# The recurrent mixer on compact operands: two 64x64 products at the diagonal quarters in place of one block-diagonal 128x128 product

## The chip, the cores and the metric

One core of one Trainium2 chip runs the whole program. The metric is the device time of one execution in microseconds. Smaller is better. Three executions of the kernel before gave a median of 4775.67 us.

## The reference, cut to what matters

The program is two layers of one kind (not touched here) and then a second block. In the second block one of the two branches is a recurrent mixer with 16 heads of 64 channels, run forwards and backwards over 768 tokens (256 of context, 512 of the sequence). Per head and per direction it computes, token by token (`w` is the decay, `a` and `b` the rank-one correction, `k`, `v`, `r` as usual):

```
S_t = S_(t-1) * w_t  +  (S_(t-1) a_t) b_t^T  +  v_t k_t^T        # 64 x 64 state of a head
y_t = S_t r_t                                                    # 64 outputs, used for the 512 tokens of x
```

The outputs of both directions are added, normalised per head, a bonus term is added, and the result is gated. The kernel computes this in chunks of 64 tokens: inside a chunk a triangular system is solved, between chunks a 64x64 state per head is carried. All operands of this part are f32.

## The kernel before, in words

`rwkv_phase` (L1896 on) does the recurrent mixer. Two heads share the 128 partitions, so 16 heads make 8 pairs, and with two directions there are 16 units. One unit has 12 chunks (`NCH`), of which the first 4 (`CCH`) are context and give no output. The loop over `ITERATIONS` runs a software pipeline: in one iteration unit u is built (`solve`, `fill`), unit u-1 is scanned (`scan`), unit u+1 is prepared on VectorE and ScalarE (`prepare`, `open_lora`, `exps`), and the operations of a pair of heads (`norm_product`, `tile_product`, `final_product`) are spread over even and odd iterations. Each iteration has 36 slots. The order of the work on each engine is written out slot by slot: in each slot TensorE does `solve`, then `fill` (slots 3 to 11), then `scan`, then at most one operation of the others. Everything waits on counted semaphores.

What each part does in a unit:

- `solve`: in slots 0 to 2 the gram products of four chunks each (L2062, against `qr`: 64 columns for context chunks, 128 for the others). Then five levels of the triangular solve. A level takes six slots: three batches of four products (L2079), which ScalarE copies out of PSUM (L2272), and three batches of four products (L2090), which VectorE merges under a mask (L2444, L2447) and turns (L2464). That is 60 products of each of the two kinds in a unit.
- `fill`: four gram products with k (L2105), then four transposes of `wb` (L2110), four of `wk` (L2115), for each of three batches.
- `scan`: three slots for each of the 12 chunks. Slot one makes W (L2130, and L2133 against the state), ScalarE copies it (L2288). Slot two makes N (L2137), ScalarE copies it (L2291) and also scales the old state (L2295). Slot three makes the state's increment (L2154, L2157), and VectorE combines it with the scaled old state (L2412, L2415). For the 8 output chunks slot three has three products more (L2148, L2149, L2160). They give rows of outputs, which VectorE copies or adds (L2475, L2478) and TensorE turns back once for each pair of heads (L2225).

Every product of two heads is one product of the full 128x128 array: the stationary operand holds the two heads at its diagonal quarters and zeros elsewhere (`wb`, `wk`, `wq`, `wV`, `wAT`, `wBT`, `wS` and so on). The zeros are set once by GpSimd (L1860) in the phase before, and the wide copies keep them. An f32 product is two records in the trace (two weight loads and two matmuls). An f32 transpose is one record of each.

Of the kernel before, what the change touches and what calls it, by code (L numbers as in the profile page):

```python
# [15 lines left out]
P = 128  # L16
# [1775 lines left out]
class MixerSpill(Side):  # L1792
# [5 lines left out]
        "heads_spilled", "constants_loaded", "zeroed", "share_kept", "mean_ready", "root_taken", "inverse_ready", "rows_scaled"]  # L1798
# [9 lines left out]
    def bind(self, landed, *sems):  # L1808
        self.landed = landed
        self.slot_spilled = sems[:self.SLOTS]  # L1810
        (self.heads_spilled, self.constants_loaded, self.zeroed, self.share_kept, self.mean_ready, self.root_taken, self.inverse_ready,
         self.rows_scaled) = sems[self.SLOTS:]
# [42 lines left out]
    def gpsimd(self, pool):  # L1855
# [3 lines left out]
        for n in ("wb", "wk", "wq", "wV"):  # L1859
            nc.gpsimd.memset(R[n][:], 0.0).then_inc(self.zeroed, 1)  # L1860
# [7 lines left out]
        pool.wait_ge(self.zeroed, 4)  # L1868
# [27 lines left out]
def rwkv_phase(nc, T, R, lora, gd, ob_d, weights, chunks, last_stored):  # L1896
# [12 lines left out]
    qr, wq, wb, wk, wV = R["qr"], R["wq"], R["wb"], R["wk"], R["wV"]  # L1909
    X, U, wAT, Y = R["X"], R["U"], R["wAT"], R["Y"]  # L1910
    wBT, wbt, wkt, Cc, Dd = R["wBT"], R["wbt"], R["wkt"], R["C"], R["D"]
    wS, wP, wW, wN, pl = R["wS"], R["wP"], R["wW"], R["wN"], R["pl"]
    bonus, rk, rows, yb, sq, ob = R["bonus"], R["rk"], R["rows"], R["yb"], R["sq"], R["ob"]
# [4 lines left out]
    def flat(ap):  # L1918
        return ap.rearrange("p h t -> p (h t)")

    def flat4(ap):
        return ap.rearrange("p c h t -> p (c h t)")

    def wide4(ap):
        return ap.rearrange("p c (o t) -> p c o t", o=1).to_broadcast([P, 4, 2, L_CH])

    def level(d, lv):
        return cst["level"][:, d, lv, :].bitcast(U32).rearrange("p (c h t) -> p c h t", c=1, h=2).to_broadcast(
            [P, 4, 2, L_CH])

    def strict(d):
        return cst["strict_wide"][:, d, :].rearrange("p (c h t) -> p c h t", c=1, h=2).to_broadcast([P, 4, 2, L_CH])

    def incl(d):
        return cst["incl"][:, d, :].rearrange("p (c t) -> p c t", c=1).to_broadcast([P, 4, L_CH])

    def four(bank):
        return psum[:, bank, :].rearrange("p (c h t) -> p c h t", c=4, h=2)

    def r_slot(u):  # L1940
        return 1 + u % 3

    def two(ap, u, c):

        return ap[:, u % 2, c:c + 2].rearrange("p c t -> p (c t)")

    def slot_of(ap, u):
        return ap[:, u % 2]
# [23 lines left out]
    PRESET_AT = {16: 0, 27: 1, 35: 2}  # L1972
    preset_order = ((0, 1, 2), (0, 2, 1))

    def solve_step(k):
# [6 lines left out]
             "s_ready", "y_ready", "norm_sums", "bonus_sums", "v_turned", "rows_turned", "mean_ready", "var_ready",  # L1982
             "gate_ready",
             "opened", "exps_ready", "q_widened", "y_preset", "u_copied", "bt_copied", "kt_copied", "w_copied",
             "n_copied", "s_copied", "s_decayed", "squared", "norm_roots", "v_copied", "ln_root",
             "sums_ready", "less_ready", "b_ready", "a_ready", "k_ready", "q_ready", "r_ready", "wb_ready", "wk_ready",
             "pl_ready", "y_opened", "at_ready", "d_ready", "x_opened", "x_done", "y_back", "y_final", "gram_k_read",
             "y_taken", "kr_ready", "kk_ready", "rk_ready", "bonus_ready", "yb_ready", "centred", "sq_ready",
             "normed", "inverse_ready", "ln_inverse", "scaled", "added", "ob_ready", "pads_zero", "weights_loaded"]
    with Phase(nc, names) as (  # L1990
            block, rk_loaded, v_loaded, up_loaded, ob_stored0, ob_stored1,
            lora_up, gram_b, gram_k, b_turned, k_turned, u_ready, z_ready, w_ready, n_ready,
            s_ready, y_ready, norm_sums, bonus_sums, v_turned, rows_turned, mean_ready, var_ready,
            gate_ready,
            opened, exps_ready, q_widened, y_preset, u_copied, bt_copied, kt_copied, w_copied,
            n_copied, s_copied, s_decayed, squared, norm_roots, v_copied, ln_root,
            sums_ready, less_ready, b_ready, a_ready, k_ready, q_ready, r_ready, wb_ready, wk_ready,
            pl_ready, y_opened, at_ready, d_ready, x_opened, x_done, y_back, y_final, gram_k_read,
            y_taken, kr_ready, kk_ready, rk_ready, bonus_ready, yb_ready, centred, sq_ready,
            normed, inverse_ready, ln_inverse, scaled, added, ob_ready, pads_zero, weights_loaded):  # L2000
        ob_stored = (ob_stored0, ob_stored1)

        @block.gpsimd
        def _(pool):
            nc.gpsimd.memset(qr[:, :, N_ALL:], 0.0).then_inc(pads_zero, 1)
            nc.gpsimd.memset(Cc[:, :, XCH, :], 0.0).then_inc(pads_zero, 1)
            nc.gpsimd.memset(Dd[:, :, XCH, :], 0.0).then_inc(pads_zero, 1)
# [38 lines left out]
        def _(pe):  # L2046
            def solve(k, u):

                g, d = divmod(u, 2)
                if k < 3:  # L2050
                    b = k
                    pe.wait_ge(wb_ready, 2 * u + 2)
# [4 lines left out]
                    for i in range(4):  # L2057
                        c = 4 * b + i
                        at = slice(c * L_CH, (c + 1) * L_CH)
                        rhs = qr[:, 0, at] if c < CCH else qr[:, 0:r_slot(u) + 1:r_slot(u), at]  # L2060
                        n = L_CH if c < CCH else P
                        last = nc.tensor.matmul(psum[:, b, i * P:i * P + n], flat(wb[:, c]), rhs, start=True, stop=True)  # L2062
# [6 lines left out]
                if step == 0:  # L2069
# [7 lines left out]
                    for i in range(4):  # L2077
                        c = 4 * b + i
                        last = nc.tensor.matmul(psum[:, b, i * P:(i + 1) * P], flat(wAT[:, c]), flat(X[:, c]),  # L2079
                                                start=True, stop=True)  # L2080
                    last.then_inc(u_ready, 1)
                else:
# [3 lines left out]
                    for i in range(4):  # L2086
                        c = 4 * b + i
                        y = flat(Y[:, u % 2, c])
                        l_, r_ = (y, flat(U[:, c])) if lv < LEVELS else (flat(U[:, c]), y)
# [157 lines left out]
            for i in ITERATIONS:  # L2247
                build, scanned, prep, norm, tile, final = stages(i)
                for k in range(SLOTS_):
# [4 lines left out]
                    if scanned is not None:  # L2254
                        scan(k, scanned)
# [1403 lines left out]
```

## Time and profile before

| | us |
|---|---|
| median of three executions | 4775.67 |
| lowest and highest | 4772.65, 4778.11 |
| span of the profiled execution | 4773.1 |
| of it: stretch 2070 to 3170, the recurrent mixer | 1100 |
| one pair of units in it (two iterations) | 130.2 |

The profiled execution is one run, 2.6 us under the median. A row of the profile names the line, the engine, the operation and its tiles, how often it occurs, its busy time as a union over time, and the mean duration of one. PE is TensorE's matmuls, PEld its weight loads, DVE is VectorE, ACT is ScalarE, POOL is GpSimd. Matmuls overlap in the pipeline, so the duration of one (275 ns) is longer than the distance from one to the next.

### The profile page before, as it was taken

Reading aid. Unit: us, or ns where it says so; the run is one execution under the profiler, and the core shown is the slowest. Engines: PE = TensorE matmul, PEld = TensorE weight load, DVE = VectorE, ACT = ScalarE, POOL = GpSimd, SP = SyncE. Lnnn points to the kernel's source line nnn. Section 1 sums busy time; section 2 is a strip of 40 time slices with the busy share of each in tenths; the row PEclk is TensorE's granted clock in tenths of the full one; section 3 lists DMA queues with packets and bytes.
Section 4 is the critical chain, followed back from the end, with each engine's and each line's share of the span. In section 5 each row is a group of like instructions: output and inputs, shape, how many; then the busy total and the mean of one; then the engine's idle time right before and its main releaser. Section 6 shows DMA issues by size and latency. Waiting matters only on the chain. (4 is left out here: it accounts for less than half of the span.)

```text
span 4773.1 us, 57369 instructions
## 1 busy us (share of the span) xinstructions
PE 4295.2 (90%) x20622; PEld 3153.4 (66%) x20622; DVE 3084.4 (65%) x6230; ACT 1654.8 (35%) x3360; POOL 850.6 (18%) x866
## 2 busy tenths in 40 slices
PE   8989999989998999989999999989899887777777
PEld 6657887747887877879888888968644333333332
DVE  5664434674434767567777777634577888888885
ACT  3354233353242356135555455432211111111111
POOL 1101010101011012000000000000134444444443
PEclk9999999999998999989999999989999988999989
DMA  4213433213433102310000000033599999999998
GB/s 131 67 40 128 146 124 98 82 40 106 148 126 117 62 18 97 103 36 12 15 11 7 15 15 15 1 132 111 197 388 416 421 413 413 413 411 415 409 415 345
DMA packets 150587, 794.50 MB, mean 166 GB/s; under 512 B 19880, under 2 KB 23192, under 8 KB 83488
## 3 DMA queue, kind: packets, MB, share of 16 engines
q0 software_dynamic: 84544, 575.18, 29.9%
q1 hardware_dynamic: 58272, 188.32, 12.0%
q10 hardware_dynamic: 7488, 27.30, 1.8%
q8 instruction: 169, 2.77, 0.2%
q14 instruction: 114, 0.93, 0.1%
HBM read 766.53 MB, written 20.00 MB: 165 GB/s over the span
## 5 line engine op out<-in xcount | busy, mean ns | idle before, releaser
L3255 PE MATMUL psum<-rows,diag 128*128 128x512 f32 x2048 | 1003.6, 640 | 228.1 <-ACT diag L3134 209.4
L3255 PEld LDWEIGHTS psum<-rows,diag 128*128 128x128 f32 x2048 | 408.3, 204 | 779.8 <-issue 766.8
L2996 DVE SCALAR_TENSOR_TENSOR uh<-rows,h_rows 128x1024 f32<-128x1024 f32 x512 | 628.3, 1227 | 205.1 <-DMA rows<-in_peer_uv,sel_idx 178.6
L2953 POOL DMA_INDIRECT rows<-in_peer_uv,sel_idx x512 | 611.2, 1194 | 739.0 <-PE psum L3255 677.4
L529 DVE TENSOR_TENSOR w_split_lo<-w_raw,w_split_hi 128x1024 fp32r<-128x1024 f32 (+1 forms) x271 | 325.0, 1209 | 498.8 <-ACT w_split_hi L516 494.7
L516 ACT CAST w_split_hi<-w_raw 128x1024 fp32r<-128x1024 f32 (+1 forms) x271 | 276.5, 1028 | 616.2 <-PE psum L465 397.3
L3127 ACT ACTIVATE g<-g 128x4 f32<-128x4 f32 x128 | 26.3, 205 | 1090.2 <-DVE g L3007 1090.2
L2079 PE MATMUL psum<-x,wAT_wide 128*128 128x128 f32 x1920 | 254.5, 276 | 1.4 <-DVE x L2444 1.0
L2079 PEld LDWEIGHTS psum<-x,wAT_wide 128*128 128x128 f32 x1920 | 237.4, 192 | 18.4 <-issue 15.0
L693 POOL TENSOR_TENSOR uT_lo<-normed_rows,uT_hi 128x512 fp32r<-128x512 f32 x64 | 90.2, 1409 | 664.8 <-ACT uT_hi L669 664.8
L465 PE MATMUL psum<-hT_mlp_hi,w_split_hi 128*128 128x512 f32 x512 | 201.1, 393 | 4.7 <-DVE hT_mlp_lo L261 4.6
L2090 PE MATMUL psum<-x,Y_wide 128*128 128x128 f32 x1536 | 202.1, 275 | 0.0
L465 PE MATMUL psum<-hT_mlp_hi,w_split_lo 128*128 128x512 f32 x512 | 200.3, 391 | 0.0
L465 PE MATMUL psum<-hT_mlp_lo,w_split_hi 128*128 128x512 f32 x512 | 200.2, 391 | 0.0
L465 PE MATMUL psum<-w_split_hi,uT_hi 128*128 128x512 f32 x512 | 199.2, 389 | 0.0
L465 PE MATMUL psum<-w_split_lo,uT_hi 128*128 128x512 f32 x512 | 199.2, 389 | 0.0
L465 PE MATMUL psum<-w_split_hi,uT_lo 128*128 128x512 f32 x512 | 199.2, 389 | 0.0
L2650 POOL DMA_DIRECT2D merge_stage<-hT_spill x7 | 3.7, 538 | 1094.9 <-POOLq L190 1090.7
L2090 PEld LDWEIGHTS psum<-x,Y_wide 128*128 128x128 f32 x1536 | 189.4, 192 | 10.8 <-issue 9.8
L2272 ACT COPY x<-psum 128x512 f32<-128x512 f32 x240 | 140.6, 586 | 156.0 <-PE psum L2079 152.5
L3134 ACT ACTIVATE diag<-ident_sb,g 128x128 f32<-128x128 f32 x512 | 163.5, 390 | 36.7 <-DVE g L3012 36.7
L2412 DVE SCALAR_TENSOR_TENSOR wS<-psum,pl,wP 128x128 f32<-128x128 f32 x160 | 54.9, 343 | 170.5 <-PE psum L2157 170.4
(538 smaller groups left out, 9356.7 us busy)
## 6 DMA issues: line engine op xcount, KB each, us to landing
w_raw<-in_w_in SPq DMA_DIRECT2D x105, 512.0 KB, 4.3
w_raw<-in_w_up SPq DMA_DIRECT2D x64, 512.0 KB, 4.2
w_raw<-in_w_down SPq DMA_DIRECT2D x64, 512.0 KB, 4.2
amask_sb<-in_w_mod ACTq DMA_DIRECT2D x48, 512.0 KB, 4.5
wq<-in_peer_wq SPq DMA_DIRECT2D x24, 512.0 KB, 7.7
rows<-in_peer_uv,sel_idx POOLq DMA_INDIRECT x512, 12.6
qkpad<-in_w_out SPq DMA_DIRECT2D x12, 512.0 KB, 5.1
w_raw<-in_w_out SPq DMA_DIRECT2D x12, 512.0 KB, 3.9
```

The source lines that it names most:

```text
L465: last = nc.tensor.matmul(psum[0:rows, bank, 0:cols], l_, r_, start=(start and c == 0 and j == 0), stop=(stop and c == len(pairs) - 1 and ...
L516: nc.scalar.copy(ring.hi[:, q % SPLIT_RING, :, 0:w], slot(q)[:, :, 0:w]).then_inc(hi_ready, 1)
L529: nc.vector.tensor_tensor(ring.lo[:, q % SPLIT_RING, :, 0:w], slot(q)[:, :, 0:w], ring.hi[:, q % SPLIT_RING, :, 0:w].bitcast(F32), ALU.sub ...
L693: return nc.gpsimd.tensor_tensor(uT.lo[:, k, :], squares[:, k % 2, :], uT.hi[:, k, :].bitcast(F32), ALU.subtract)
L2079: last = nc.tensor.matmul(psum[:, b, i * P:(i + 1) * P], flat(wAT[:, c]), flat(X[:, c]), start=True, stop=True)
L2090: last = nc.tensor.matmul(psum[:, b, i * P:(i + 1) * P], l_, r_, start=True, stop=True)
L2272: nc.scalar.copy(flat4(U[:, batch(b)]), psum[:, b, :]).then_inc(u_copied, 1)
L2412: nc.vector.scalar_tensor_tensor(wS[:], psum[:, 5, 0:P], scale, wP[:], ALU.mult, ALU.add).then_inc(s_copied, 1)
L2953: nc.gpsimd.indirect_dma_start(out=rows[:, n % RB, :], out_offset=None, in_=I["peer_uv"], in_offset=bass.IndirectOffsetOnAxis(ap=sel[:, t, ...
L2996: nc.vector.scalar_tensor_tensor(prod[:], rows[:, n % RB, 0:D], 1.0, h[:, t, :], ALU.mult, ALU.mult, accum_out=dots[:, (n // BATCH) % 2, s ...
L3134: nc.scalar.activation(diag[:, n % (2 * BATCH), :], ident[:], ACT.Copy, scale=g2[:, b % 2, i:i + 1]).then_inc(diag_ready, 1)
L3255: last = nc.tensor.matmul(psum[:, 2 * (t % 2) + half, :], diag[:, n % (2 * BATCH), :], rows[:, n % RB, D + half * NB:D + (half + 1) * NB], ...
```

## The change

Each product of two heads becomes two products of 64x64 operands (`by_head`): partitions 0 to 63 against 0 to 63, and partitions 64 to 127 against 64 to 127. No operand holds the zero quarters any more, so every tile of the mixer is half as wide and the copies, masks and turns work on 256 columns where they worked on 512.

- The gram products, the solve and the scan use `by_head`. The transposes of `wb` and `wk` become `by_head` products against an identity (`cst["eye"]`).
- The state's decay: one more product (identity against the old state) adds the old state in PSUM, and ScalarE scales the sum while it copies it. VectorE's `state` and ScalarE's scaling of the old state are gone.
- The outputs are made channels first, with `vv`, the state and N as stationary operands, and are accumulated over both directions in PSUM bank 6. The rows, their copies and their turning are gone. ScalarE copies bank 6 once for each pair of heads.
- ScalarE's widening of q and its presets of Y are gone. GpSimd presets Y. GpSimd's zeroing is gone.
- In each slot TensorE and ScalarE do `scan` ahead of `solve`. `qr` and `Ss` have more buffers, and some waits on `y_done` and `n_copied` are new.

```diff
+    def by_head(out, lhsT, rhs, start, stop):
+        for at in halves:
+            last = nc.tensor.matmul(out[at], lhsT[at], rhs[at], start=start, stop=stop)
+        return last
...
         @block.gpsimd
         def _(pool):
-            nc.gpsimd.memset(qr[:, :, N_ALL:], 0.0).then_inc(pads_zero, 1)
...
+            for u in range(UNITS):
+                for j, b in enumerate(scan_order[u % 2]):
+                    if u >= 2:
+                        pool.wait_ge(n_ready, 12 * (u - 2) + 4 * j + 4)
+                    nc.gpsimd.tensor_copy(Y[:, u % 2, batch(b)], mask(cst["eye"])).then_inc(y_preset, 1)
...
-                        last = nc.tensor.matmul(psum[:, b, i * P:i * P + n], flat(wb[:, c]), rhs, start=True, stop=True)
+                        last = by_head(psum[:, b, i * P:i * P + n], wb[:, c], rhs, True, True)
...
-                        last = nc.tensor.matmul(psum[:, b, i * P:(i + 1) * P], flat(wAT[:, c]), flat(X[:, c]),
-                                                start=True, stop=True)
+                        last = by_head(psum[:, b, i * L_CH:(i + 1) * L_CH], AT[:, c], X[:, c], True, True)
...
-                        last = nc.tensor.matmul(psum[:, b, i * P:(i + 1) * P], l_, r_, start=True, stop=True)
+                        last = by_head(psum[:, b, i * L_CH:(i + 1) * L_CH], l_, r_, True, True)
...
-                        last = nc.tensor.transpose(psum[:, 3, i * P:(i + 1) * P], flat(wb[:, 4 * b + i]), ident[:])
+                        last = by_head(psum[:, 3, i * L_CH:(i + 1) * L_CH], wb[:, 4 * b + i], cst["eye"], True, True)
...
-                    last = nc.tensor.matmul(W, flat(wBT[:, u % 2, c]), v, start=True, stop=(n == 0))
+                    last = by_head(W, BT[:, u % 2, c], v, True, n == 0)
...
-                    nc.tensor.matmul(N, flat(Y[:, u % 2, c]), wW[:], start=True, stop=True).then_inc(n_ready, 1)
+                    by_head(N, Y[:, u % 2, c], Ww[:], True, True).then_inc(n_ready, 1)
...
+                        by_head(S_, kt[:, u % 2, c], v, True, False)
+                        if n:
+                            by_head(S_, cst["eye"], Ss[:, n % 2], False, False)
+                        pe.wait_ge(n_copied, 12 * u + n + 1)
+                        by_head(S_, bt[:, u % 2, c], Nn[:], False, True).then_inc(s_ready, 1)
                     if n >= CCH:
...
+                        by_head(y, vv[:, g % 2, c], Cc[:, u % 2, x_], first, False)
+                        by_head(y, Ss[:, n % 2], qr[:, u % 3, 1, at], False, False)
+                        pe.wait_ge(n_copied, 12 * u + n + 1)
+                        by_head(y, Nn[:], Dd[:, u % 2, x_], False, last_).then_inc(y_done, 1)
...
-                    for c in range(XCH):
-                        last = nc.tensor.transpose(psum[:, 7, c * L_CH:(c + 1) * L_CH], rows[:, c * P:(c + 1) * P],
-                                                   ident[0:L_CH, 0:L_CH])
...
-                    nc.scalar.copy(flat4(U[:, batch(b)]), psum[:, b, :]).then_inc(u_copied, 1)
+                    nc.scalar.copy(flat(U[:, batch(b)]), narrow(b)).then_inc(u_copied, 1)
...
-                        nc.scalar.activation(wP[:], wS[:], ACT.Copy, scale=pl[:, u % 3, c:c + 1]
-                                             ).then_inc(s_decayed, 1)
...
+                    act.wait_ge(s_ready, 11 * u + n + 1)
+                    nc.scalar.activation(Ss[:, (n + 1) % 2], psum[:, 5, 0:L_CH], ACT.Copy, scale=pl[:, u % 3, c:c + 1]
+                                         ).then_inc(s_copied, 1)
...
-                    nc.vector.scalar_tensor_tensor(wS[:], psum[:, 5, 0:P], scale, wP[:], ALU.mult, ALU.add
-                                                   ).then_inc(s_copied, 1)
...
-                    nc.vector.copy_predicated(X[:, batch(b)], level(d, lv), four(b)).then_inc(x_done, 1)
+                    nc.vector.copy_predicated(X[:, batch(b)], level(d, lv), cells(narrow(b))).then_inc(x_done, 1)
...
-                    nc.vector.transpose(flat4(Y[:, u % 2, batch(b)]), flat4(X[:, batch(b)])).then_inc(y_back, 1)
+                    nc.vector.transpose(flat(Y[:, u % 2, batch(b)]), flat(X[:, batch(b)])).then_inc(y_back, 1)
```

## Rows read from the trace of the kernel before

**Rows 1.** Page: the span, then busy time, share and records of each engine.
```profile
span 4773.1 us, 57369 instructions
PE 4295.2 (90%) x20622; PEld 3153.4 (66%) x20622; DVE 3084.4 (65%) x6230; ACT 1654.8 (35%) x3360; POOL 850.6 (18%) x866
```

**Rows 2.** Stretches, all engines: start:end, length, busy (records), clock, DMA share, GB/s.
```profile
2070.00:3170.00 1100.00, 1004.20 (x8028) 932.08 (x8028) 791.90 (x1224) 550.28 (x1216) 4.34 (x10) 0.98 0.05 16
...
2662.30:2729.00 66.70, 61.33 (x499) 57.02 (x499) 49.72 (x78) 32.50 (x72) 0.00 (x0) 1.00 0.02 5
2729.00:2792.60 63.60, 60.60 (x502) 57.37 (x501) 48.03 (x74) 35.50 (x81) 0.00 (x0) 1.00 0.07 22
```

**Rows 3.** Timeline of PE in one unit: start, length, line, form, records merged.
```profile
2662.35 1.00 PE L2062 MATMUL psum<-qr,arena 128*128 128x64 f32 x8
2663.19 0.44 PE L2130 MATMUL psum<-arena,wBT_wide 128*128 128x128 f32 x2
...
2666.78 0.60 PE L2180 MATMUL psum<-lora,arena 128*128 128x256 f32 x2
2667.21 1.05 PE L2079 MATMUL psum<-x,wAT_wide 128*128 128x128 f32 x8
...
2671.70 0.60 PE L2110 MATMUL psum<-ident_sb,arena 128*128 128x128 f32 x4
...
2672.36 1.02 PE L2180 MATMUL psum<-lora,arena 128*128 128x512 f32 x2
2673.22 1.05 PE L2079 MATMUL psum<-x,wAT_wide 128*128 128x128 f32 x8
```

**Rows 4.** Timeline around products with 64 stationary rows, then their weight loads' group.
```profile
2684.24 0.39 PE L2133 MATMUL psum<-wS,arena 128*128 128x128 f32 x2
2684.56 0.71 PE L2225 MATMUL psum<-ident_sb,y_rows 64*128 64x64 f32 x8
2685.20 1.05 PE L2079 MATMUL psum<-x,wAT_wide 128*128 128x128 f32 x7
...
L2225 PEld LDWEIGHTS psum<-ident_sb,y_rows 64*128 64x128 f32 x64 | 4.6, 138 | 1.8 <-DVE y_rows L2478 1.0
```

**Rows 5.** Waits, longest in total, over 12 units (2208.1 to 2989.5): total, times, longest.
```profile
PE psum L2133 <- DVE wS L2412: 18.0, 24, 1.4
```

**Rows 6.** Timeline of PE in the last unit, which has no solve beside its scan.
```profile
3117.50 0.49 PE L2133 MATMUL psum<-wS,arena 128*128 128x128 f32 x2 [0.22 <-DVE wS L2412]
3118.34 0.49 PE L2137 MATMUL psum<-wW,Y_wide 128*128 128x128 f32 x2 [0.35 <-ACT wW L2288]
...
3120.12 0.49 PE L2133 MATMUL psum<-wS,arena 128*128 128x128 f32 x2 [0.22 <-DVE wS L2412]
```

**Rows 7.** Groups of VectorE and ScalarE in the mixer: count, busy us, mean ns.
```profile
L2444 DVE COPY_PREDICATED x<-arena,psum 128x512 f32<-128x512 uint32 x192 | 138.1, 719 | 34.1 <-PE psum L2090 33.6
L2464 DVE STREAM_TRANSPOSE Y_wide<-x 128x512 f32<-128x512 f32 x192 | 135.9, 708 | 4.6
L2412 DVE SCALAR_TENSOR_TENSOR wS<-psum,pl,wP 128x128 f32<-128x128 f32 x160 | 54.9, 343 | 170.5 <-PE psum L2157 170.4
...
L2455 DVE TENSOR_TENSOR wBT_wide<-psum,arena 128x512 f32<-128x512 f32 x48 | 32.2, 671 | 14.5 <-PE psum L2105 14.5
...
L2457 DVE TENSOR_TENSOR gate_rows<-psum,arena 128x256 f32<-128x256 f32 x32 | 13.1, 411 | 0.0
...
L2272 ACT COPY x<-psum 128x512 f32<-128x512 f32 x240 | 140.6, 586 | 156.0 <-PE psum L2079 152.5
...
L2321 ACT ACT_TABLE_LOAD x16 | 20.5, 1283 | 5.8 <-DVE arena L2527 5.6
```

**Rows 8.** GpSimd: the zeroing before the mixer, and the nearest copy-like operation.
```profile
1869.12 7.91 POOL L1860 MEMSET arena<- 128x1536 f32 x4
1883.38 0.57 POOL L1863 DMA_DIRECT2D zr_spill<-z_ring  x1 [6.34 <-DVE z_ring L3390]
...
L693 POOL TENSOR_TENSOR uT_lo<-normed_rows,uT_hi 128x512 fp32r<-128x512 f32 x64 | 90.2, 1409 | 664.8 <-ACT uT_hi L669 664.8
```

More of the change, by code:

```diff
@@ L1908, in rwkv_phase @@
     kk, kr, nrm, dec, Lc, eR, aa = (R[n] for n in ("kk", "kr", "nrm", "dec", "Lc", "eR", "aa"))
[L1909 to L1913, printed above, removed]
+    qr, wb, wk, vv = R["qr"], R["wb"], R["wk"], R["v"]
+    X, U, AT, Y = R["X"], R["U"], R["AT"], R["Y"]
+    BT, bt, kt, Cc, Dd = R["BT"], R["bt"], R["kt"], R["C"], R["D"]
+    Ss, Ww, Nn, pl = R["S"], R["W"], R["N"], R["pl"]
+    bonus, rk, yb, sq, ob = R["bonus"], R["rk"], R["yb"], R["sq"], R["ob"]
+    halves = (slice(0, 64), slice(64, P))
     def cells(ap):
@@ L2249, in _ @@
                 for k in range(SLOTS_):
+                    if scanned is not None:
+                        scan(k, scanned)
                     if build is not None:
@@ L2381, in _ @@
                 for k in range(SLOTS_):
+                    if scanned is not None:
+                        scan(k, scanned)
                     if build is not None:
@@ L2385, in _ @@
                             fill(k, build)
-                    if scanned is not None:
-                        scan(k, scanned)
-                    if build is not None and k in (1, 3):
-                        widen_q(k // 2, build)
                     if prep and k in (0, 2, 4, 6):
@@ L2393, in _ @@
                         exps(k, prep)
-                    if prep is not None and k in PRESET_AT:
-                        preset(PRESET_AT[k], prep)
                     if tile is not None and k in TURNED_AT:
@@ L2603, in _ @@
                         solve(k, build)
-                    if scanned is not None and k % 3 == 2 and k < SLOTS_ - 1:
-                        state(k // 3, scanned)
                     if build is not None:
@@ L2609, in _ @@
                             fill(k, build)
-                    if scanned is not None and k in (24, 35):
-                        outputs(k // 35, scanned)
                     if tile is not None and k in (6, 11):
@@ L2717, in rwkv_constants @@
     incl = [(row <= col), (row >= col)]
-    out["strict_wide"] = np.stack([np.tile(m, (1, 2)) * out["ones"] for m in strict], 1).astype(f)
+    out["strict"] = np.stack(strict, 1).astype(f)
     out["incl"] = np.stack(incl, 1).astype(f)
@@ L2725, in rwkv_constants @@
         lev[:, 1, i] = 1.0 * (same & ((row // m) % 2 == 0) & ((col // m) % 2 == 1))
-    out["level"] = np.tile(lev, (1, 1, 1, 2)) * out["ones"][:, None, None, :]
+    out["level"] = lev
+    out["eye"] = (row == col).astype(f)
     tt = np.arange(N_ALL)
@@ L3367, in second_block_program @@
         for n in ("wb", "wk"):
-            R[n] = share.take([NCH, 2, L_CH])
-        for n in ("wq", "wV"):
-            R[n] = share.take([2, NCH, 2, L_CH])
+            R[n] = share.take([NCH, L_CH])
+        R["v"] = share.take([2, NCH, L_CH])
         loads = [(cst[n][:], I["rwc_" + n]) for n in cst] + [
```

260 lines of the change are left out of this document (97 added, 163 removed).

## The prediction

> **What bounds the kernel now.** The page is read first: PE is busy for 90% of the span, but that is an average over stages [rows 1]. The table of stretches then shows the stage that the change touches. It lasts 1100 us and has PE busy for 1004 of them, DVE for 792 and ACT for 550, with a clock of 0.98 and nearly no DMA [rows 2]. Within it two iterations, one pair of units, take 66.7 + 63.6 = 130.3 us, so one unit takes 65.15 us. PE is busy for 61.0 of these at the full clock, DVE for 48.9, ACT for 34.0 [rows 2]. The mixer is bound by PE. The phases before and behind it are separated by barriers and their code stays the same, so the whole effect is what a unit gains or loses, times 16.
>
> The timeline prices what PE does. Eight full products take 1.05 us with the last record's 0.275 in it, so one record starts 0.111 us behind the other and a product of two records costs 0.223 [rows 3]. A full transpose has one record and costs (0.60 - 0.27) / 3 = 0.109 [rows 3]. The lora product with 512 columns takes 0.86 and the one with 256 takes 0.43, start to start [rows 3]. A gram product with only 64 moving columns is no cheaper: eight records take 0.84 from start to start, 0.105 each [rows 3]. So at 64 columns it is the load of 128 stationary columns that sets the pace, and narrowing the moving side alone gains nothing.
>
> With these the unit adds up. The products of a unit are 24 gram, 60 + 60 in the solve, 23 for W, 12 for N, 22 for the state and 24 for the outputs, 225 in all: 225 x 0.223 = 50.2 us. The 24 transposes make 2.6, the four lora products 2 x (0.86 + 0.43) = 2.6. The operations of a pair of heads are five products of 512 columns and one of 256 (norms, bonus, final ones: 5 x 0.86 + 0.43 = 4.7) and 12 transposes (1.3), so 6.0, or 3.0 for a unit. Turning the output rows back takes 2685.20 - 2684.46 = 0.74 for a pair, 0.4 for a unit [rows 4]. The sum is 58.8 us. The measured 65.15 leaves 6.3 us of waits and restarts. The main named wait is W's second product on VectorE's state, 18 us over 12 units with single waits of 1.4 [rows 5].
>
> **The change part by part.**
>
> Number of records. A full product becomes two of 64x64, each of two records. So 0.223 us becomes the price p of four short records. It is counted as follows: 8 gram products with 64 columns, 120 of the solve, 24 former transposes, 23 of W, 12 of N, 22 + 10 of the state (the identity product is new, for all but the first and last chunk) and 24 of outputs make 243 pairs at p. The 16 gram products with 128 moving columns cost q.
>
> The price p. No row shows two quarters of the array at work, so it is bounded. Above: the records follow one another. The nearest row is the turning with 64 stationary rows and 64 moving columns. Its weight loads are busy for 4.6 us in 8 groups of 8, so (0.575 - 0.138) / 7 = 0.062 apart [rows 4], and p = 4 x 0.062 = 0.248. The column count gives nearly the same: 0.43 for two records of 256 columns is 0.054 for 64 [rows 3], p = 0.216 to 0.248. Below: the second head's records run in the other quarter beside the first head's, p = 2 x 0.062 = 0.124. A lower end still is one record's time for all, 0.062, which would need both halves of one f32 product side by side in one quarter, and I leave it out, since they use the same cells. Break-even: with waits as now and the terms below, 65.15 - 6.3 - 5.6 - 1.7 = 51.55 = 243p + 16 x 1.8p gives p = 0.189. So the sign hangs on this one price. I take 0.124 to 0.135: the two products share no row and no column of the array, and rows show that a weight load is hidden behind a matmul even within one group of 64 rows, since 0.062 holds both [rows 4].
>
> The Trainium skill (TensorEngine Tiling (Array Packing), Key Properties) says that different tiles can load weights and multiply in parallel. That is the side of 0.124; no row here shows it.
>
> Solve, scan, fill and gram: 243 x 0.13 = 31.6, and 16 pairs at 2 x 0.111 = 0.223, 3.6 (0.446 if nothing overlaps).
>
> Switches. Before and behind the only group with 64 stationary rows the trace shows a gap: the two records of L2133 fill 0.22 from 2684.24, but the next group begins 0.10 later; its eight records at 0.062 fill 0.50 of the 0.64 until the next full product, 0.14 over [rows 4]. A visit to another shape thus costs 0.2 both ways. In the changed unit the short shape is the rule, and the full-array groups are 4 lora products and, for a pair of heads, 2 norm, 1 bonus, 3 turns of v and 3 final ones, 8.5 groups a unit: 8.5 x 0.2 = 1.7 us. The bounds are 0 (if switches hide in waits) and 3. The skill's same section states that changing the mode drains the engine; the trace agrees, with its 0.1 on each side [rows 4].
>
> Lora and the pair's products stay: 2.6 + 3.0. The turning goes, -0.4.
>
> VectorE and ScalarE. Copies, masks and turns of 512 columns fall to 256. The nearest pair of rows is 671 ns for 512 and 411 for 256 [rows 7], so 0.26 to 0.36 saved for each. DVE has 18 masked copies (719), 15 turns (708) and 6 masks a unit: 39 x 0.3 = 11.7, and the state's 11 x 0.343 = 3.8, the rows' two copies 1.3, half of the wide wb and wk 1.9: DVE falls from 49 to about 30 us. ACT loses half of 21 copies of 0.586 [rows 7] (5), the presets (1.9), the widening (1.7), the decay scaling (4.1), and takes on the state copy, 11 x 0.3 = 3.3: about 25 us. Neither binds. These savings are worth nothing while PE binds. They matter for what is late next.
>
> GpSimd. The zeroing of 7.9 us goes. It is hidden: POOL then sits idle for 6.34 us until VectorE's tile [rows 8], worth 0. The new presets, 48 of 256 columns, have as nearest row 1.4 us for 512 columns with two inputs [rows 8]; at 0.4 to 1.4 each, 1 to 4 us a unit, on an engine with nothing else, an iteration ahead of use: 0. The upper cost is a slower VectorE beside it, within the range.
>
> New waits. N's copy on ScalarE now waits for the output products of the chunk before (`y_done`). PE issued those a slot and a half earlier, so it is met; behind it ScalarE has queued the U copies of the solve. VectorE's mask of D waits for the scan two units back: met. In the last slots the first W waits for N's last copy of the unit before, which is now exposed for some 0.8 us.
>
> What is late next. The last unit has no solve, and its rows show the bare chain: W at 3117.50, N at 3118.34, next W at 3120.12, so 0.84 us for a stage and 2.62 for a chunk [rows 6], 31.4 a unit. The short chain is about 0.75 a stage (smaller copies). PE's own work in a slot would be about 1.1 us, of which the solve's four pairs are 0.5. So a stage of 0.75 against 0.5 + 0.13 behind it stands open for 0.1 to 0.2 in most slots, 36 x 0.15 = 5 us, and a table load of 1.28 on ScalarE [rows 7] ahead of a copy costs up to a microsecond three times a unit. The waits of 6.3 become about 9.
>
> Sum for a unit: 31.6 + 3.6 + 5.6 + 1.7 + 9 = 51.5. Gain 13.6 us, times 16 = 218. First units and the last scan shift this by less than 10. From the profiled 4773 that is 4555; the profiled run is within 0.1% of the median, so I say 4555.
>
> **The rivals.**
>
> *The records follow one another.* Either the quarters' weight loads pass through one path, or the issue of a load and a matmul needs about the 0.062 that the smallest row shows, whatever the tile. For it: at 64 columns the present kernel is already bound by weight loads and not by columns [rows 3], and no row shows two at once. Against it: the disjoint quarters. Then 243 x (0.216 to 0.248) = 52.5 to 60.3, 16 x 0.446 = 7.1, + 5.6 + 1.7 + 5 of waits = 71.9 to 79.7, +6.8 to +14.6 a unit, 4882 to 5007, middle 4950. It decides from p = 0.189 on. The skill (TensorE: Matmul & The Clock Gate, Back-to-back issue gap) has a rule of this kind: with its hardware decoder off, the sequencer needs about 62 ns for each matmul. By it p is 0.248, as the upper row.
>
> *Overlap, but the chain binds.* Waits on ScalarE's longer queue or a lower clock in a thinner PE (clock 1.00 in full units [rows 2]) take back half: 58 us a unit, 4660. For it: the chain of 0.84 a stage and single waits of 1.4 already now [rows 5, 6].
>
> *Nothing changes.* p near 0.19 by partial overlap: 4773 within 10.
>
> **How the numbers follow.** Overlap as forecast (4490 to 4620): 0.42. Chain-bound or partial overlap (4620 to 4765): 0.15. Within 0.2% (about what a measurement of this kernel can tell from no change): 0.05. One after another: 0.38. The likeliest one's own range is 4490 to 4620. Leaving out 0.07 below 4500 and 0.08 above 4985, the range is 4500 to 4985. Faster 0.57, same 0.05, slower 0.38.
>
> **What the profile after would show.** Four short records of a pair in 0.125 us or in 0.22 to 0.25: this is the main step. PE busy for about 42 us a unit against 61. Gaps of 0.1 around the lora products. The unit at 51 us, with waits for ScalarE's W and N copies on top. DVE at 30 and ACT at 25 us a unit. If a unit is over 65 with PE without gaps, the forecast has failed at p. If p holds and the unit is near 58, it has failed at the waits.

## The result and the profile after

The changed kernel takes 4489.8 us (4476.3 to 4496.3, four runs) against 4774.2 for the kernel before in the same series: a ratio of 0.9400, 95% interval 0.9383 to 0.9417. That is 284 us less, where 218 were forecast. The time lies 10 us under the lower end of the range.

The profile page of the changed kernel, with the lines that answer to [rows 1]:

```profile
span 4494.6 us, 74705 instructions
PE 4000.6 (89%) x29550; PEld 2823.7 (63%) x29550; DVE 2819.5 (63%) x5982; ACT 1519.4 (34%) x3304; POOL 867.1 (19%) x908
```

PE's share of the span is 89% where it was 90%, so the page alone tells nothing of the gain. The stage does. First the mixer of the kernel before, from one barrier's records to the next, in the columns of [rows 2]:

```profile
2070.10:3161.00 1090.90, 996.55 (x7993) 925.62 (x7993) 785.47 (x1216) 544.15 (x1208) 0.60 (x3) 0.98 0.05 15
```

Then the same stage of the changed kernel, and eight whole units of it:

```profile
2068.20:2873.40 805.20, 710.10 (x16921) 597.35 (x16921) 520.87 (x968) 408.66 (x1152) 28.52 (x48) 0.96 0.07 21
2316.70:2697.60 380.90, 344.03 (x8452) 290.34 (x8449) 259.87 (x485) 203.67 (x577) 14.47 (x24) 1.00 0.06 20
```

The stage goes from 1090.9 to 805.2 us, 285.7 less. The whole span falls by 4773.1 - 4494.6 = 278.5, so all else, phases whose code is nearly the same, took 7 us more. That is within what these phases vary by. A unit takes 380.90 / 8 = 47.6 us instead of 65.15. In it PE is busy for 43.0 us, DVE for 32.5, ACT for 25.5 and POOL for 1.8.

PE's timeline inside a unit, to be read against [rows 3]: start, length, line, form, records merged.

```profile
2502.22 0.28 PE L1937 MATMUL psum<-arena,kt_cells 64*64 64x64 f32 x4
2502.34 0.28 PE L1937 MATMUL psum<-S_cells,arena 64*64 64x64 f32 x4
...
2502.92 0.63 PE L1937 MATMUL psum<-x,AT 64*64 64x64 f32 x16
2503.39 0.28 PE L1937 MATMUL psum<-arena,BT_cells 64*64 64x64 f32 x4
...
2508.49 1.13 PE L2167 MATMUL psum<-lora,arena 128*128 128x512 f32 x2
2509.54 0.33 PE L1937 MATMUL psum<-W_cells,Y_cells 64*64 64x64 f32 x4
2509.71 1.04 PE L1937 MATMUL psum<-qr,arena 64*64 64x128 f32 x16
```

Sixteen short records take 2503.39 - 2502.92 = 0.47 us, and each group of four, which is one pair of heads' products, takes 0.1165. The starts of single records, which this view merges, show how: the second head's record starts 7 ns behind the first head's, and the next one 51 ns after that. Each quarter starts a record every 58.3 ns, and the two quarters work at the same time. With 128 moving columns (the last row) the starts of the 16 records are 0.109 apart in each quarter, so a pair of heads takes 0.219 and the quarters gain next to nothing over the full product's 0.223. The lora product at 2508.49 takes 1.05 us to its successor where it took 0.86 [rows 3].

Groups of VectorE, ScalarE and GpSimd, for [rows 7, 8]:

```profile
L2403 DVE COPY_PREDICATED x<-arena,psum 128x256 f32<-128x256 uint32 x192 | 83.3, 434 | 113.8 <-PE psum L1937 113.4
L2424 DVE STREAM_TRANSPOSE Y_cells<-x 128x256 f32<-128x256 f32 x192 | 85.5, 445 | 6.6
L2253 ACT COPY x<-psum 128x256 f32<-128x256 f32 x240 | 89.6, 373 | 67.0 <-PE psum L1937 65.2
L2281 ACT ACTIVATE S_cells<-psum,pl 128x64 f32<-128x64 f32 x176 | 54.8, 311 | 74.7 <-PE psum L1937 74.7
L1998 POOL COPY Y_cells<-arena 128x256 f32<-128x256 f32 x48 | 28.5, 600 | 710.0 <-PE psum L1937 692.7
```

The waits of PE in the eight units, for [rows 5]: total, times, longest.

```profile
PE psum L1937 <- ACT S_cells L2281: 16.8, 15, 1.4
PE psum L1937 <- ACT W_cells L2269: 10.0, 12, 1.9
PE psum L2216 <- DVE sq L2508: 4.8, 4, 1.2
PE psum L1937 <- DVE x L2403: 2.9, 4, 0.7
PE psum L1937 <- DVE gate_rows L2417: 1.1, 4, 0.3
```

These are 35.6 us in eight units, 4.5 a unit. The first is on the state copy that the change moved from VectorE to ScalarE.

### The profile page after: what moved, and what is told of

It is laid out like the page before. It is cut to its first block and busy times, and to the rows that moved or that the text cites. A ratio compares the mean times of both kernels' runs of the same rounds, so it can differ in the third digit from the quotient of the medians.

```text
span 4494.6 us, 74705 instructions
## 1 busy us (share of the span) xinstructions
PE 4000.6 (89%) x29550; PEld 2823.7 (63%) x29550; DVE 2819.5 (63%) x5982; ACT 1519.4 (34%) x3304; POOL 867.1 (19%) x908
## 5 line engine op out<-in xcount | busy, mean ns | idle before, releaser
L1998 POOL COPY Y_cells<-arena 128x256 f32<-128x256 f32 x48 | 28.5, 600 | 710.0 <-PE psum L1937 692.7
L1937 PE MATMUL psum<-x,AT 64*64 64x64 f32 x3840 | 154.2, 220 | 7.6 <-DVE x L2403 7.3
L2403 DVE COPY_PREDICATED x<-arena,psum 128x256 f32<-128x256 uint32 x192 | 83.3, 434 | 113.8 <-PE psum L1937 113.4
L3111 PE MATMUL psum<-hT_p,wq 128*128 128x128 f32 (+2 forms) x384 | 136.7, 469 | 6.3 <-ACT hT_p L2996 3.7
L1937 PEld LDWEIGHTS psum<-x,AT 64*64 64x64 f32 x3840 | 132.9, 136 | 13.0 <-DVE x L2403 9.9
L465 PE MATMUL psum<-hT_all_hi,w_split_hi 128*128 128x512 f32 (+1 forms) x352 | 123.0, 350 | 1.8 <-DVE w_split_lo L529 1.8
L465 PE MATMUL psum<-hT_hi,w_split_hi 128*128 128x512 f32 x272 | 110.2, 405 | 14.5 <-DVE hT_lo L261 7.5
```

The source lines that it names most:

```text
L465: last = nc.tensor.matmul(psum[0:rows, bank, 0:cols], l_, r_, start=(start and c == 0 and j == 0), stop=(stop and c == len(pairs) - 1 and ...
L1937: last = nc.tensor.matmul(out[at], lhsT[at], rhs[at], start=start, stop=stop)
L1998: nc.gpsimd.tensor_copy(Y[:, u % 2, batch(b)], mask(cst["eye"])).then_inc(y_preset, 1)
L2403: nc.vector.copy_predicated(X[:, batch(b)], level(d, lv), cells(narrow(b))).then_inc(x_done, 1)
L3111: return nc.tensor.matmul(psum[:, bank, tokens], wq[:, n % WR, c, :], hT[:, c, tokens], start=(c == 0), stop=(c == DC - 1))
```

## The experiments

Each is an edit of the changed kernel. Beside the ratio to the kernel before stands the length of the mixer stage, from the same two barriers as above; the changed kernel has 0.9400 and 805.2. Outside the stage the profiled executions differ by up to 11 us, so small differences are read from the stage. A stage is that of one profiled execution each, so a difference of a few us between two stages is not told from none.

### Is it the overlap of two quarters?

**e1_head_after_head.** A batch's four products go out head by head instead of head beside head. The edit in short:

```diff
-    for i in range(4):
-        last = by_head(out(i), lhsT(i), rhs(i), True, True)
+    for at in halves:
+        for i in range(4):
+            last = nc.tensor.matmul(out(i)[at], lhsT(i)[at], rhs(i)[at], start=True, stop=True)
```

> The changed kernel, but each batch of four solve products goes head after head: four products of the first quarter, then four of the second, where the heads alternated. The same records, the same work. Theory (two quarters work at once, and only neighbours in the queue that lie in different quarters do): 16 records no longer overlap, a batch costs 0.93 us where it cost 0.466, 30 batches a unit make 14 us, 16 units 223 us: 4490 + 223 = 4713. Rival (a 64x64 record is simply cheaper, 0.029 each whatever its neighbour is): 4490, no change.

Measured: 0.9526 (0.9507 to 0.9545), stage 868.3, so +63: neither theory (223 or nothing). PE's timeline of this kernel (L1944 is the reordered batch, L1937 the products behind it in the program):

```profile
2501.45 0.74 PE L1944 MATMUL psum<-x,Y_cells 64*64 64x64 f32 x13
2501.97 0.27 PE L1937 MATMUL psum<-arena 64*64 64x64 f32 x1
2502.03 0.22 PE L1944 MATMUL psum<-x,Y_cells 64*64 64x64 f32 x1
2502.08 0.22 PE L1937 MATMUL psum<-arena 64*64 64x64 f32 x1
2502.09 0.22 PE L1944 MATMUL psum<-x,Y_cells 64*64 64x64 f32 x1
```

Records of the later products start before the last ones of the batch ahead of them. The rows do not name the quarter, but the starts fall on two grids of 58 ns. The first quarter has finished its eight records and goes on to the next group, while the second still works off its own. So the two quarters are two queues, each with 58 ns a record, and one may run ahead of the other. That gives a third theory: what TensorE needs for its work is set by how many records each quarter has, not by which stand side by side.

The 63 us need a second reason, as the counts are unchanged. From the first start of a batch to its last are 0.70 us here and 0.415 in the changed kernel, so whoever waits for a batch gets it 0.28 later. For 480 batches that would be 134 us if all of it were paid. That it is what the 63 us consist of is not shown.

**e9_extra_in_one_quarter** and **e11_extra_in_turn.** Every solve product is issued in three parts instead of two. In e9 the third part is always the first head's; in e11 it changes from product to product. Both write the same values again, and both have the same number of records.

```diff
-        for at in halves:
+        for at in (halves[0], halves[0], halves[1]):          # e9
+        for at in (halves[i % 2], halves[0], halves[1]):      # e11
```

> The changed kernel, but each of the 120 solve products of a unit is issued as three 64x64 products: head 0, head 0 again (same result in the same place), head 1. Theory (each quarter is a queue of its own, one record of 64 columns takes it 0.058 us, and the fuller quarter sets the time): the fuller quarter's work for a product goes from 0.117 to 0.233, 14 us a unit, less what waits absorb: +190 to +224 us, 4680 to 4714. Rival (a record costs 0.029 wherever it lies): half as many records more, +7 us a unit, +80 to +112 us.

> The twin of e9 with exactly as many records: the extra product is head 0's for even chunks and head 1's for odd ones. Theory (two queues with a window of several records): the quarters share the extra work, 0.175 for a product, +7 us a unit less what waits absorb: +80 to +112 us, 4570 to 4602, and some 110 us under e9. Rival (neighbours alone overlap, or records have one price): no difference to e9.

Measured: e9 0.9747 (0.9727 to 0.9766), stage 971.1; e11 0.9558 (0.9538 to 0.9578), stage 874.9. Their stretches over the stage:

```profile
2067.60:3038.70 971.10, 913.40 (x20760) 810.52 (x20760) 527.15 (x968) 412.19 (x1151) 24.43 (x48) 0.96 0.06 18
```

```profile
2068.60:2943.50 874.90, 806.06 (x20761) 704.59 (x20761) 523.40 (x968) 412.15 (x1152) 27.60 (x48) 0.97 0.07 20
```

And PE's timeline around one batch, of e9 and then of e11:

```profile
2501.07 1.09 PE L1943 MATMUL psum<-x,AT 64*64 64x64 f32 x24
2501.99 0.67 PE L1937 MATMUL psum<-arena 64*64 64x64 f32 x16
```

```profile
2500.65 0.91 PE L1943 MATMUL psum<-x,AT 64*64 64x64 f32 x24
2501.35 0.68 PE L1937 MATMUL psum<-qr,arena 64*64 64x64 f32 x16
```

The same 24 records take 0.92 in e9, about 16 times 58.3 ns, and 0.70 in e11, 12 times 58.3 ns: what the fuller quarter has. With the same count of records in the stage, one quarter's queue made longer costs 166 us, and both made longer by half of that costs 70. Each quarter is a queue: this is shown. Both costs are below the ranges expected (190 to 224, and 80 to 112); they are 96 us apart where some 110 were expected. The full price of 1920 extra parts at 0.1165 would be 224, and half of it 112, so some 40 to 60 us of the extra work lay in waits that were there before.

### What does a change of shape cost?

**e2_full_visit** and **e3_short_visit.** Behind each of the 192 N products stands one idle operation that nothing waits for: in e2 a full transpose of one record, in e3 a pair of 64x64 products.

```diff
                     by_head(N, Y[:, u % 2, c], Ww[:], True, True).then_inc(n_ready, 1)
+                    nc.tensor.transpose(psum[:, 5, 256:384], ident[:], ident[:])                # e2
+                    by_head(psum[:, 5, 256:320], cst["eye"], cst["eye"], True, True)            # e3
```

> The changed kernel with one idle transpose of the full array (128x128, result unread) behind each N product of the scan, 192 in all. Theory (a visit to another shape drains the array on both sides, 0.195 beside the work of 0.109): 192 x 0.304 = 58 us if TensorE binds throughout, about 45 where it falls into waits: 4535 to 4548 in all. Rival (switches cost nothing of their own): 192 x 0.109 = 21, at most 4511.

> The twin of e2: one idle pair of 64x64 products (identity against identity, result unread) at the same 192 places. Theory (a pair costs 0.117 and no switch): 192 x 0.117 = 22 us if TensorE binds throughout, 15 with waits: 4505 to 4512, and some 35 us under e2. Rival (TensorE no longer binds, the chain of copies does): 0 to 5 us.

Measured: e2 0.9520 (0.9499 to 0.9540), stage 857.6, +52.4, so 0.273 us each; e3 0.9400 (0.9382 to 0.9419), stage 810.5, +5.3, so 0.028 each. For e2 the theory held, at the upper end of what it gave. For e3 it failed (15 to 22 us) and the rival held: the 5 us are hardly told from nothing. PE's timeline of e2 around one of them:

```profile
2400.85 0.33 PE L1937 MATMUL psum<-W_cells,Y_cells 64*64 64x64 f32 x4
2401.11 0.33 PE L2130 MATMUL psum<-ident_sb 128*128 128x128 f32 x1
2401.37 0.68 PE L1937 MATMUL psum<-x,Y_cells 64*64 64x64 f32 x16
```

One full record takes 0.26 us to its successor, 0.15 over its own 0.109 [rows 3]. Starts of single records show another 0.149 from the last short one to it, where 0.05 is usual between short ones. So the switch there and back is 0.25, and the times of the two runs say about the same: 0.273 - 0.028 = 0.245. The work of one record is small beside it. And e3 holds a second result: a pair whose records take 0.1165 costs at most some 0.03 at this place. There TensorE has time to spare.

### Are TensorE's records the bound?

**e5_no_decay_product.** It leaves out the state's product with the identity, and so the carry of the state from chunk to chunk.

```diff
-                        if n:
-                            by_head(S_, cst["eye"], Ss[:, n % 2], False, False)
```

> The state's product with the identity, which the change adds for ten chunks of a unit, is left out, and with it the carry of the state from chunk to chunk. Theory A, TensorE's records set the time: ten pairs at 0.1165 us are 1.17 us a unit, 19 us in 16 units. Theory B, TensorE has slack and the chain of chunk after chunk sets the pace: these records fill a wait, 0 to 5 us.

Measured: 0.9392 (0.9377 to 0.9408), stage 803.2: 2 us less for 160 pairs, 0.013 each, not told from nothing and far from the 19 of theory A. Theory B's figure holds: these records lie in time in which TensorE would wait anyway. That it is the chain from W to N to the state that makes this time is not shown. The extra parts of e11 in the solve cost 70 / 960 = 0.073 a pair, much more but also less than their 0.1165. PE is busy for 43 of 47.6 us and still is not what every record has to pay for.

### What are the other engines' savings worth?

**e6_vector_load** and **e12_half_vector_load.** Idle products of 512 columns on VectorE, two or one behind each of the solve's 12 turns in a unit. That makes 24 added operations a unit in e6 and 12 in e12. Where the text on e12 speaks of 24 turns and masked copies, the places are the 12 turns. That text gives 8.1 us a unit; 124.7 / 16 = 7.8 were measured. Each idle product also waits for the one before it (not shown below).

```diff
                     nc.vector.transpose(flat(Y[:, u % 2, batch(b)]), flat(X[:, batch(b)])).then_inc(y_back, 1)
+                    for _ in range(2):                                       # e12: range(1)
+                        nc.vector.tensor_tensor(R["junk"][:], levels_flat, levels_flat, ALU.mult)
```

> The changed kernel with VectorE's removed work given back: two extra products of 128x512 elements behind each turn of the solve (result unread), 12 x 2 a unit, about 16 us a unit, which brings VectorE back to some 48 us a unit. Theory (the shorter unit of 47.6 us needs a light VectorE): VectorE now binds, +3 to +8 us a unit, +50 to +130 us. Rival (VectorE's halved copies are worth nothing even now): within 10 us of 4490.

> The change with one extra idle 128x512 product on VectorE behind each of the 24 turns and masked copies of the solve in a unit; the run with two of them had 673 ns each, 16.2 us a unit, and was 166.7 us slower than the change. Here it is half, 8.1 us a unit, which takes VectorE from 32.5 to 40.6 busy us in a unit of 47.6. Theory A, VectorE binds only once it is nearly full: at 40.6 of 47.6 nearly nothing is lost, under 30 us, and the 167 of the full load come from its second half. Theory B, each delay behind a turn or mask lies in the solve's own chain of waits, long before the engine is full: the loss goes with the load, 70 to 100 us.

Measured: e6 0.9753 (0.9734 to 0.9773), stage 977.5; e12 0.9532 (0.9516 to 0.9548), stage 868.6. The added group and the stage, of e12 and then of e6:

```profile
L2431 DVE TENSOR_TENSOR idle_copy<-arena 128x512 f32<-128x512 f32 x192 | 124.7, 649 | 0.0
```

```profile
2063.00:2931.60 868.60, 732.00 (x16920) 610.26 (x16921) 629.73 (x1160) 409.57 (x1152) 22.64 (x48) 0.94 0.06 20
```

```profile
L2431 DVE TENSOR_TENSOR idle_copy<-arena 128x512 f32<-128x512 f32 x384 | 258.5, 673 | 6.6
```

```profile
2064.50:3042.00 977.50, 772.24 (x16920) 639.96 (x16921) 759.33 (x1352) 410.39 (x1152) 23.26 (x48) 0.90 0.06 17
```

The first 125 us of load cost 63, half of themselves, with VectorE busy for only 630 of 869 us. So it is not a knee near the full engine: the "nothing until it is full" of theory A has fallen (under 30 us). The 63 us are also under theory B's 70 to 100. The second 134 us cost 109, so the price rises as the engine fills; strictly linear is wrong too. The 172 us of e6 are over the 50 to 130 that were expected.

Part of the price goes by way of TensorE's clock. The granted clock of the stage is 0.94 in e12 and 0.90 in e6 against 0.96, and PE, with the same 16921 records, is busy for 22 and 62 us more than the 710 of the changed kernel. The other 41 and 110 us are added idle time of PE. That an operation behind a turn delays the solve's next step is the likely reason for it; no run places the load elsewhere.

Taken together, putting back about what the change took from VectorE (16 us a unit) takes 172 of the 286 us away. The load stands behind the turns only, while the savings lie in copies, masks and turns, so 172 is an estimate of their worth and not a measurement.

### The order of scan and solve in a slot

**e4_solve_first, e13_order_scalar_only, e14_order_tensor_only.** The change also turned the order in a slot: the scan's operations now stand ahead of the solve's, on TensorE and on ScalarE. e4 puts the old order back on both, e13 on ScalarE alone, e14 on TensorE alone.

```diff
-                    if scanned is not None:
-                        scan(k, scanned)
                     if build is not None:
                         solve(k, build)
                         if 3 <= k < 12:
                             fill(k, build)
+                    if scanned is not None:
+                        scan(k, scanned)
```

> The changed kernel with the old order in a slot on TensorE and ScalarE: solve and fill first, then scan. Theory (the order is worth little, the gain is the price of a pair): within 5 us of 4490, the chain's waits move from S to other places. Rival (scan first is what keeps the chain hidden in short slots): 2 to 4 us of waits more a unit, +30 to +60 us, 4520 to 4550.

> The change with the old order of a slot (solve, then scan) on ScalarE alone; TensorE keeps scan before solve. The old order on both engines gained 19 us. Theory A, the cost of the new order lies in ScalarE's queue, where the solve's copies wait behind a scan copy whose product is not there yet: the gain is there with this half, 15 to 20 us. Theory B, it lies in TensorE's queue, which stands at a scan product with the solve's products ready behind it: this half gains under 5 us or loses, and the other half has the gain.

> The change with the old order of a slot (solve, then scan) on TensorE alone; ScalarE keeps scan before solve. Theory A, the cost of the new order lies in ScalarE's queue: under 5 us gained, or a loss, as TensorE issues W after the solve while ScalarE waits for W's result first. Theory B, it lies in TensorE's queue: 15 to 20 us gained.

Measured: e4 0.9355 (0.9339 to 0.9370), stage 785.9, 19 less; e13 0.9591 (0.9575 to 0.9607), stage 894.0, 89 more; e14 0.9410 (0.9394 to 0.9426), stage 808.8, 4 more, which is not told from no change. No theory on e4 gave a gain of 19, and of those on e13 and e14 none held for both. Waits over eight units (2340.6 to 2769.1) of e13, PE's and then ScalarE's:

```profile
PE psum L1937 <- ACT S_cells L2281: 33.7, 48, 1.3
PE psum L1937 <- ACT W_cells L2269: 17.1, 28, 1.3
PE psum L1937 <- ACT N_cells L2276: 12.7, 36, 0.4
```

```profile
ACT x L2253 <- PE psum L1937: 104.6, 112, 2.7
```

And of PE in e4 (2312.9 to 2684.3):

```profile
PE psum L1937 <- ACT kt_cells L2262: 9.0, 8, 1.1
PE psum L1937 <- ACT S_cells L2281: 4.8, 7, 0.9
```

Neither queue alone holds the 19 us. In e13 ScalarE stands at the solve's copy, whose products TensorE issues only after the scan's; meanwhile TensorE waits for the scan's copies behind it. The copies of S, W and N come late for 63.5 us in eight units. Disagreement as such is not the matter: the other mismatch, e14, costs 4 us over the change and 23 over e4. Of the two orders that agree solve-first is the better one. The wait on the state falls from 16.8 to 4.8, while one of 9.0 on kt's copy is new. What in the scan-first order makes S late is not settled. The long ScalarE operations at a slot's end would do it, and no run tests that alone.

### A better version

**e10_solve_first_short_sums.** e4, and the sums over a head's 64 rows and the turns of v also as quarter pairs, so that fewer full-array visits are left. It also copies each batch of v in one ScalarE operation in place of two or three.

```diff
+    def head_sums(out, rhs):
+        for at in halves:
+            last = nc.tensor.matmul(out[at], cst["ones"][at, at], rhs[at], start=True, stop=True)
+        return last
...
-                    nc.tensor.matmul(psum[:, 7, :], cst["ones"][:], sq[:], start=True, stop=True).then_inc(var_ready, 1)
+                    head_sums(psum[:, 7, :], sq).then_inc(var_ready, 1)
```

> A version that may beat both: e4's order (solve first), and the sums over a head's channels and the turns of v also as pairs of 64x64 stationary operands, so that 8 of the 17 full-array visits of a pair of heads are gone; one copy in place of two or three for each batch of v. Theory (a visit costs 0.2 to 0.25 beside its work): 64 visits x 0.2 to 0.25 = 13 to 16 us under e4, 4455. Rival (TensorE waits for copies anyway, drains hide there): within 4 us of e4, 4467 to 4475.

Measured: 0.9326 (0.9311 to 0.9342), 4452.8 us, stage 775.7. It is 10 us under e4 in the stage, between the theory (13 to 16) and its rival (under 4), and the two intervals of the ratio overlap slightly. How much of the 10 us the 64 visits carry and how much the 32 ScalarE copies that are gone is not told apart. In the whole time it is 37 us under the change (4489.8), the fastest of all.

## Why the prediction was right and wrong

The sign and the mechanism held: the two heads' products overlap, and the rival of one record after another is out. The size was 66 us too small. The step that failed is the price p, put at 0.130 us for a pair of heads where 0.1165 was measured. By the terms of the sum, for a unit:

**The price p** is the mis-sized term. The forecast took 0.130 from two weight loads at 0.062 [rows 4]; the trace has 0.1165, from 0.0583 a record. 243 x 0.0135 = 3.3 us, so 52 us over 16 units. The error was to treat 0.062 as a floor. It came from loads of 64 rows by 128 columns, and the quarter's load has 64 columns; whether that makes the difference no run tests. The lower bound of 0.124 was therefore no bound. With p at that bound and all else as forecast the sum gives 4532, with the measured p it gives 4503. So most of the miss is p, and the last step out of the range comes from the other terms below.

The Trainium skill (TensorE: Matmul & The Clock Gate, Back-to-back issue gap) gave the sequencer about 62 ns for each matmul with its hardware decoder off. Here four records start in 0.1165 us, 29 ns each, so that rule does not bind in this kernel. The same page of the Trainium skill (Part 3, The mechanism) has matmuls start and end strictly in program order. The starts in e1 show that order inside a quarter and not between quarters.

**Gram pairs** with 128 moving columns took 0.219 for 0.223: 3.5 us for 3.6. **The full-array work** stayed at 5.6.

**Switches.** 8.5 visits a unit were counted, as the trace has them. The forecast had 0.2 each. Single starts show 0.195 from a product's first record to its successor above the time of before, as forecast, and 0.09 ahead of it that was not counted: 0.29 for the seven products. The one and a half turns have 0.585 to their successor for 4 x 0.109, with the 0.09 ahead 0.24. That makes 2.4 us for 1.7. e2 against e3 gives 0.245.

**Waits.** The rest is 47.6 - 28.3 - 3.5 - 5.6 - 2.4 = 7.8 us for 9 forecast, worth 19 us. The profile names 4.5 of them, 3.4 on ScalarE's S and W copies. The forecast named W and N; no row of N's is in the list above, and S is the largest.

Together: 52 + 19 - 11 (switches) + 2 (gram) = 62 us of the 66, as (51.5 - 47.6) x 16 = 62. The rest lies in the first units and the last scan, or in what runs vary by. This splits the time by TensorE's own records; e3, e5 and e11 show that a record added or taken away alone does not carry its full price.

**The chain.** A stage of 0.75 was expected. The last unit after, whose rows answer to [rows 6], and its stretch:

```profile
2842.34 0.42 PE L1937 MATMUL psum<-S_cells,qr 64*64 64x64 f32 x4
2843.07 0.48 PE L1937 MATMUL psum<-W_cells,Y_cells 64*64 64x64 f32 x4 [0.31 <-ACT W_cells L2269]
...
2844.98 0.42 PE L1937 MATMUL psum<-S_cells,qr 64*64 64x64 f32 x4
```

```profile
2841.50:2847.50 6.00, 5.38 (x90) 4.86 (x89) 0.00 (x0) 1.79 (x7) 0.00 (x0) 0.50 0.00 0
```

A chunk takes 2.64 us, as the 2.62 of before. But the granted clock is 0.50 here, that is 1.2 GHz, while it was 1.00 in the rows of before. Ahead of the fall, at about 2835.4, TensorE sat idle between its short records: it was busy for 2.57 of 4.05 us. At the full clock stand the chunks just ahead of the fall and one at the end of the chain:

```profile
2831.35:2835.40 4.05, 2.57 (x44) 1.74 (x44) 0.00 (x0) 1.46 (x6) 0.00 (x0) 1.00 0.77 236
```

```profile
2832.80 0.33 PE L1937 MATMUL psum<-S_cells,qr 64*64 64x64 f32 x4 [0.36 <-ACT S_cells L2281]
2833.44 0.33 PE L1937 MATMUL psum<-W_cells,Y_cells 64*64 64x64 f32 x4 [0.31 <-ACT W_cells L2269]
2834.83 0.33 PE L1937 MATMUL psum<-S_cells,qr 64*64 64x64 f32 x4 [0.30 <-ACT S_cells L2281]
...
2856.30 0.33 PE L1937 MATMUL psum<-W_cells,Y_cells 64*64 64x64 f32 x4 [0.31 <-ACT W_cells L2269]
2858.34 0.33 PE L1937 MATMUL psum<-W_cells,Y_cells 64*64 64x64 f32 x4 [0.31 <-ACT W_cells L2269]
```

A chunk takes 2.03 and 2.04 us there for 2.62 before. The step from W to N (2832.80 to 2833.44) takes 0.64 for 0.84 before and 0.75 forecast. Twelve chunks would be 24.4 us (an estimate), half of a unit's 47.6. So the bare chain does not fill a unit, and the rival's 58 us a unit did not come. What sets the 47.6 in a full unit is not settled: e3 and e5 show slack where records of the scan stand, e12 and e6 a price of delay on VectorE.

**VectorE's and ScalarE's savings.** The busy times came as worked out: 32.5 for 30 and 25.5 for 25. The sentence behind them failed: they were put at nothing while PE binds. By e12 and e6 a load of half of VectorE's saving costs 63 us and one of the whole about 172. The sum did not need it because it was made with the waits given, 9 us; that these came out at 7.8 hangs on a light VectorE. For ScalarE's saving there is no such run. It was said that these savings matter for what is late next; they should have been priced as the condition of the 9 us.

**GpSimd.** The presets take 600 ns, 1.8 us a unit, inside the 0.4 to 1.4 taken, and nothing in the eight units waits for them: 0, as forecast. **N's new wait** on `y_done` cost nothing that shows: no wait of TensorE on N's copy is in the list of the eight units.

**The order in a slot** was not priced. The new one costs 19 us against the old one on both engines (e4).

## What to carry to other kernels

Block-diagonal operands can be replaced by quarter products: here four records of two disjoint quarters took 0.1165 us where two full ones took 0.223. Both sides had to be narrow. A record took 0.105 with 128 stationary and 64 moving columns [rows 3], 0.109 in its quarter with 64 and 128, and 0.058 with 64 and 64. Balance the records of the quarters, since each quarter is a queue of its own (166 us against 70 for the same number of records), and keep full-array work in few groups at 0.2 to 0.3 us a visit. An engine that is off the bound can still carry the gain: price its saving by the delay of the step that waits behind it. And try the orders of dependent work in the queues: of the four tried here the best and the worst are 108 us apart in the stage.

## What the hardware showed that was not expected

- Two diagonal quarters start records 7 ns and 51 ns apart in turn, 58.3 ns a record in each, and a quarter that is behind does not hold the other (e1: a later product's record at 2501.97, an earlier one's at 2502.09).
- A visit to the full array from quarter work costs 0.245 us beyond its work (e2 and e3). A product of two records of 512 columns takes 1.05 instead of 0.86 to its successor.
- VectorE's masked copy and turn of 256 columns take 434 and 445 ns, 0.60 and 0.63 of the 719 and 708 for 512 [rows 7], so halving the columns does not halve them.
- In the last unit, with the scan's short records alone, the granted clock was 0.51 from 2840.00 to 2856.20, where the last unit of before, with full records, had 1.00 from 3117.4 to 3122.8.
